# A fourth seven-product pair in each feed-forward layer, alternating PSUM quarters, and transposes one slab behind the square

## The chip, the cores and the metric

The kernel runs on one core of a Trainium2 chip. The metric is the device time of one execution in microseconds (us); for the kernel before, three runs are shown below. One execution was taken with the hardware profiler, and all rows of a trace come from it.

## What is computed

The reference is two residual blocks over 256 tokens of width 2048, in float32. What the change touches is the feed-forward part of the first block's two layers:

```python
D_MODEL = 2048
SEQ = 256
D_FF = 4 * D_MODEL
...
def squared_relu_mlp(h, w1, w2):
    z = jax.nn.relu(h @ w1)
    return (z * z) @ w2
...
        x = x + jnp.concatenate([token_out, mem_out], axis=-1) @ w_out[i]
        x = x + squared_relu_mlp(rms_norm(x, ffn_norm[i]), w_ff1[i], w_ff2[i])
```

The rest is projections, a causal pool, cross attention over a memory, differential attention, and a second block with a gated recurrence and windowed attention.

## The kernel before

**Work.** Every weight matrix is cut into groups of 512 columns, and a group into eight slabs of 256 rows, so that a slab is a 256x512 piece of weights (512 KB). SyncE loads a slab into one of four slots of `raw`. To keep float32 accuracy each slab is split in two parts: ScalarE writes `whi` (a rounded copy, `hi`, L1086) and VectorE writes `wlo` (the rest, `lo`, L1457). The activations lie split in the same way in `set0` and `set1`. TensorE then multiplies high by high, low by high and high by low (L2093 to L2095): for two tiles of rows and two blocks of 128 tokens that is 12 matmuls of 128x512 for a slab. The sums stand in PSUM in `acc0` and `acc1`, in turn by group.

**Order.** `plan()` lists the groups and puts each further step (a sum, a copy, a transpose) behind a numbered slab of an engine. `number_all` makes one stream of tasks of it, and SyncE, ScalarE, VectorE and TensorE all walk through this stream. A task is one load, one split on ScalarE, one split on VectorE, and its matmuls. The load of task n waits until VectorE has split task n-4 (`w_lo`), since there are four slots, and ScalarE's split of task n waits until TensorE has multiplied task n-4.

**The feed-forward part** (`ffn`) has four chunks of 2048 hidden columns a layer. A chunk has four groups of the first product (`w_ff1`), whose outputs are scaled, passed through the relu and squared, transposed, split and stored in `set1`, and four groups of the second (`w_ff2`), which add to `x`.

**Seven-product pairs.** In chunks 1 to 3 the first two groups of the first product are not computed as groups. They are a 2x2 block product (128 tokens by 1024 rows, times 1024 rows by 512 columns), done with seven block products in place of eight. Each block product is a stage (`p1`, `p2`, `p5`, `p3`, `p6`, `p7`, `p4`), each stage four part tasks of six matmuls (L2130 to L2132), and the 28 part tasks of a pair are spread between the ordinary slabs of the chunk before (`pair_of`). The weights of a stage are sums of blocks, which VectorE makes: `chain_sum` (L1472, for `p5`, `p6`, `p4`) adds a loaded block to one of four chain buffers (`qk`, `prob`, two halves of `mkv`), and `u3` (L1464, for `p7`) subtracts. VectorE does this for task n+2 right behind its split of task n, and needs the load of n+2 for it. The four stages `p6`, `p7`, `p4` and `p5` have such a sum for each part; `p1`, `p2`, `p3` have none. The results stand in the four quarters of two PSUM tensors, `tp` and `sd`:

```python
BLOCKS = {"p1": (0, 0), "p2": (1, 0), "p5": (0, 1), "p3": (1, 1), "p6": (1, 1), "p7": (0, 0), "p4": (1, 0)}
...
                ahead = sc.stream[task.n + 2] if task.n + 2 < len(sc.stream) else task
                if ahead.part and ahead.part.stage == "p7":
                    u3(ahead)
                elif ahead.part and ahead.part.stage in ("p5", "p6", "p4"):
                    chain_sum(ahead)
```

**The drain of a pair.** ScalarE copies `p1` to `first_c` and `p5` to `mixed_c`; VectorE adds `p2` and `p6`, then writes two quarters of the output (`part_n2`) and later the two others (`part_n1`). Relu and square on ScalarE, a transpose of 32x32 blocks on VectorE (`turn`, L1648), sixteen small DMAs on GpSimd that finish the transpose (`shuffle`, L1050), and the split into `set1` (`tail`, L1258 on ScalarE and L1630 on VectorE) follow, as for an ordinary group.

## Time and profile before

| | |
|---|---|
| median of 3 runs | 2959.76 us (2959.05 to 2961.48) |
| profiled execution | 2960.76 us, its span 2959.0 us |
| mean granted share of TensorE's clock | 0.998 |
| TensorE busy | 2916.3 us, 99% of the span |
| VectorE busy | 2055.5 us, 69% |
| ScalarE busy | 1616.3 us, 55% |
| GpSimd busy | 634.5 us, 21% |
| HBM read | 598.89 MB |

The busy time of an engine is a sum over its instructions; the time between the start of one matmul and the next is shorter than the duration that a row gives for one, since matmuls overlap. The views that matter beside the page are the chain that ended last, the waits of VectorE, and the windows over single stretches of the feed-forward part.

### The profile page before, as it was taken

Reading aid. Unit: us, or ns where it says so; the run is one execution under the profiler, and the core shown is the slowest. Engines: PE = TensorE matmul, PEld = TensorE weight load, DVE = VectorE, ACT = ScalarE, POOL = GpSimd, SP = SyncE. Lnnn points to the kernel's source line nnn. Section 1 sums busy time; section 2 is a strip of 40 time slices with the busy share of each in tenths; the row PEclk is TensorE's granted clock in tenths of the full one; section 3 lists DMA queues with packets and bytes.
Section 4 is the critical chain, followed back from the end, with each engine's and each line's share of the span. In section 5 each row is a group of like instructions: output and inputs, shape, how many; then the busy total and the mean of one; then the engine's idle time right before and its main releaser. Section 6 shows DMA issues by size and latency. Waiting matters only on the chain.

```text
span 2959.0 us, 35189 instructions
## 1 busy us (share of the span) xinstructions
PE 2916.3 (99%) x12996; PEld 2400.2 (81%) x12996; DVE 2055.5 (69%) x2679; ACT 1616.3 (55%) x2134; POOL 634.5 (21%) x1257
## 2 busy tenths in 40 slices
PE   8999999999999999999999999999999999999998
PEld 7888888888888778788788888888888887878887
DVE  6547777777866777876777777756557777887555
ACT  6435555555554566755555555545444446775433
POOL 0003312213043310013203122133324663100210
PEclk9999999999999999999999999999999999999999
DMA  7546777778777655556777778776876776666774
GB/s 263 165 151 203 237 248 250 246 244 255 243 223 243 205 170 164 164 174 203 228 256 253 251 242 253 246 219 211 239 216 200 219 227 190 207 206 206 249 254 157
DMA packets 358156, 649.53 MB, mean 220 GB/s; under 512 B 38624, under 2 KB 63584, under 8 KB 357216
## 3 DMA queue, kind: packets, MB, share of 16 engines
q1 hardware_dynamic: 312976, 578.89, 61.7%
q0 software_dynamic: 44432, 67.45, 7.2%
q8 instruction: 102, 1.67, 0.3%
q10 hardware_dynamic: 576, 0.94, 0.1%
q14 instruction: 70, 0.57, 0.1%
HBM read 598.89 MB, written 10.49 MB: 206 GB/s over the span
## 4 chain that ended last, share of the span: by engine, by line
PE 73%; DVE 14%; DMA 7%; ACT 4%; issue 2%; DVEq 0%; ACTq 0%
PE acc L2093 21%; PE acc L2095 21%; PE acc L2094 21%; DMA raw<-in_w_ff 6%; DVE wlo L1457 5%; ACT whi L1086 1%; DVE wlo L1450 1%; PE tp L2130 1%; PE tp L2132 1%; PE tp L2131 1%; DVE mkv L1472 1%; DVE ob L1900 1%; PE tp L2299 1%; PE sd L2193 0%; PE sd L2218 0%
## 5 line engine op out<-in xcount | busy, mean ns | idle before, releaser
L1457 DVE TENSOR_TENSOR wlo<-raw,whi 128x1024 fp32r<-128x1024 f32 x920 | 1110.7, 1220 | 548.4 <-ACT whi L1086 544.0
L2093 PE MATMUL acc<-whi,set_hi 128*128 128x512 f32 x3696 | 1459.4, 395 | 20.8 <-DVE wlo L1457 15.4
L2095 PE MATMUL acc<-whi,set_lo 128*128 128x512 f32 x3696 | 1440.3, 390 | 0.0
L2094 PE MATMUL acc<-wlo,set_hi 128*128 128x512 f32 x3696 | 1439.8, 390 | 0.0
L1086 ACT ACTIVATE whi<-raw 128x1024 fp32r<-128x1024 f32 x920 | 959.4, 1057 | 684.1 <-PE acc L2095 378.3
L2093 PEld LDWEIGHTS acc<-whi,set_hi 128*128 128x128 f32 x3696 | 694.8, 188 | 182.8 <-DVE wlo L1457 27.1
L2095 PEld LDWEIGHTS acc<-whi,set_lo 128*128 128x128 f32 x3696 | 694.5, 188 | 146.2
L2094 PEld LDWEIGHTS acc<-wlo,set_hi 128*128 128x128 f32 x3696 | 695.0, 188 | 143.3 <-issue 1.9
L1050 POOL DMA_DIRECT2D u<-u x832 | 406.8, 497 | 1447.5 <-DVE u L1648 1337.9
L1450 DVE SCALAR_TENSOR_TENSOR wlo<-raw,par,whi 128x512 fp32r<-128x512 f32 x160 | 111.7, 747 | 47.1 <-ACT whi L1089 46.3
L1089 ACT ACTIVATE whi<-raw,par 128x512 fp32r<-128x512 f32 x160 | 104.2, 715 | 22.4 <-PE acc L2095 10.9
L1050 POOL DMA_DIRECT2D kv<-kv x112 | 54.9, 499 | 173.2 <-DVE kv L1648 169.1
L1086 ACT ACTIVATE whi<-mkv 128x1024 fp32r<-128x1024 f32 x48 | 50.9, 1061 | 68.0 <-DVE mkv L1472 51.9
L1555 DVE TENSOR_TENSOR x<-acc,x 128x1024 f32<-128x1024 f32 x40 | 48.8, 1220 | 36.3 <-PE acc L2095 36.3
L1457 DVE TENSOR_TENSOR wlo<-mkv,whi 128x1024 fp32r<-128x1024 f32 x48 | 58.4, 1216 | 9.6 <-ACT whi L1086 8.9
L1472 DVE TENSOR_TENSOR mkv<-mkv,raw 128x1024 f32<-128x1024 f32 x36 | 44.0, 1223 | 29.0 <-DMA raw<-in_w_ff 28.9
L1630 DVE TENSOR_TENSOR set_lo<-u,set_hi 128x1024 fp32r<-128x1024 f32 x44 | 53.7, 1220 | 14.4 <-ACT set_hi L1264 12.2
L1648 DVE STREAM_TRANSPOSE u<-stage_b 128x512 f32<-128x512 f32 x80 | 52.0, 688 | 11.2 <-ACT stage_b L1145 11.2
L2130 PE MATMUL tp<-whi,set_hi 128*128 128x512 f32 x144 | 56.0, 389 | 0.0
L2131 PE MATMUL tp<-wlo,set_hi 128*128 128x512 f32 x144 | 56.0, 389 | 0.0
L2132 PE MATMUL tp<-whi,set_lo 128*128 128x512 f32 x144 | 56.0, 389 | 0.0
L1086 ACT ACTIVATE whi<-qk 128x1024 fp32r<-128x1024 f32 x24 | 25.5, 1062 | 48.1 <-DVE qk L1472 33.0
(332 smaller groups left out, 2121.3 us busy)
## 6 DMA issues: line engine op xcount, KB each, us to landing
raw<-in_w_ff SPq DMA_DIRECT2D x560, 512.0 KB, 4.7
raw<-in_w_in SPq DMA_DIRECT2D x248, 512.0 KB, 4.5
raw<-in_w_out SPq DMA_DIRECT2D x96, 512.0 KB, 4.4
u<-u POOLq DMA_DIRECT2D x832, 32.0 KB, 4.2
raw<-in_w_mem_kv SPq DMA_DIRECT2D x32, 512.0 KB, 4.3
raw<-in_w_proj_a SPq DMA_DIRECT2D x32, 512.0 KB, 4.7
raw<-in_w_proj_b SPq DMA_DIRECT2D x32, 512.0 KB, 6.9
raw<-in_w_kv SPq DMA_DIRECT2D x48, 256.0 KB, 3.3
```

The lines of the kernel that those rows point to most:

```text
L1050: dma(to, of).then_inc(sm["shuffled"], 16)
L1086: A_(whi[:, c], src, ACT.Copy).then_inc(w_hi, 1)
L1089: ins = A_(whi[:, c], raw[:, c], ACT.Copy, scale=gain_of(fold, SLAB_K * task.s + t))
L1450: ins = V.scalar_tensor_tensor(out=wlo[:, c], in0=raw[:, c], scalar=gain_of(fold, SLAB_K * task.s + t), in1=whi[:, c].bitcast(f32), op0=AL ...
L1457: V.tensor_tensor(wlo[:, c], src, whi[:, c].bitcast(f32), ALU.subtract).then_inc(w_lo, 1)
L1472: V.tensor_tensor(t, t, raw[:, c], ALU.add).then_inc(sm["chain_add"], 1)
L2093: T.matmul(o, h[:, tok], whi[:, c], start=first, stop=False)
L2094: T.matmul(o, h[:, tok], wlo[:, c], start=False, stop=False)
L2095: ins = T.matmul(o, l[:, tok], whi[:, c], start=False, stop=last)
L2130: T.matmul(bank, h, whi[:, c], start=first, stop=False, skip_group_check=True)
L2131: T.matmul(bank, h, wlo[:, c], start=False, stop=False, skip_group_check=True)
L2132: ins = T.matmul(bank, l, whi[:, c], start=False, stop=last, skip_group_check=True)
```

## The change

In chunks 0 to 3 of a layer the number of pairs is now 0, 1, 1 and 2 (`PAIRS`). The last chunk's first product has no ordinary groups left: two pairs take its four groups, the first over columns 0 to 1023 of the chunk (`col` 0), the second over columns 1024 to 2047. The 56 part tasks of the two lie between the slabs of chunk 2, from 21 slabs before its second product to slab 29 of the 32 of that product (28 part tasks in some 40 slabs for each pair before). Two groups of 8 slabs go and 28 part tasks come, in each of the two layers: the stream grows from 1096 to 1120 tasks, and the matmuls fall by 2 x (192 - 168) = 48. The four groups of the second product in chunk 2 and in chunk 3 are woven in another order, so that the rows of `set1` are free, or needed, in steps.

A pair with an odd number uses the PSUM quarters in another order (`bank`), so that `p1` of a pair only has to wait for `part_n2` of the pair before it, and `p5` for `part_n1`. `part_p1` waits for the relus of the pair before, since it writes `first_c` over.

The transpose of every group and pair (`turn`) now stands a slab behind the square that it reads. Before, the two stood at the same slab in chunk 0, and in the later chunks too for ordinary groups.

```diff
+FF2_LATE = ((0, 1, 2, 3), (4, 5), (6, 7))
+FF2_EVEN = ((0, 1), (2, 3), (4, 5), (6, 7))
+PAIRS = (0, 1, 1, 2)
...
+    def seven(layer, chunk, src, col, first, last):
+
+        p = sc.pair_of(layer, chunk, src, col, first, last)
+        pair = sc.pairs[p]
+        sc.at("act", pair.end("p1") + 5, "part_p1", p)
+        sc.at("dve", pair.end("p2") + 3, "part_c11", p)
+        sc.at("act", pair.end("p5") + 3, "part_p5", p)
+        sc.at("dve", pair.end("p6") + 3, "part_q", p)
+        return p
+
+    def drain(p, of, rst, z, kt, turn, split):
+
+        pair = sc.pairs[p]
+        add = pair.end("p7") + 3
+        if of == "n1":
+            add = max(pair.end("p4") + 3, add + 5)
+        sc.at("dve", add, "part_" + of, p)
+        sc.at("act", add + 2, "relu_" + of, p, rst)
+        sc.at("act", add + 2, "part_square", p, of, sc.staged, sc.tails)
+        sc.turned(max(turn, add + 3), split, ("staged", sc.staged), z, kt)
+        sc.staged += 1
+        if of == "n2":
+            sc.at("act", add + 3, "part_p7", p, sc.staged)
...
-        for c in range(NCHUNK):
-            halved = c > 0
-            gs = [sc.group(f"w_ff1{layer}", 0, D * c + GW * i, a) for i in range(2 if halved else 0, 4)]
+        waiting = []
+        for c, count in enumerate(PAIRS):
+            gs = [sc.group(f"w_ff1{layer}", 0, D * c + GW * i, a) for i in range(2 * count, 4)]
...
             for i, g in enumerate(gs):
-                turn, split = S * (g + 1) + 1, S * (g + 2) + 1
-                if halved:
-                    turn, split = S * (g + 1) + 2, S * (g + 2) + 2
-                sc.at("act", S * (g + 1) + 1, "epi_relu2", g, rst, sc.staged, sc.tails)
-                sc.at("act", turn, "epi_square", g, sc.tails)
-                sc.turned(turn, split, ("staged", sc.staged), z, 4 * i + (8 if halved else 0))
+                e = S * (g + 1)
+                late = 1 if count else 0
+                sc.at("act", e + 1, "epi_relu2", g, rst, sc.staged, sc.tails)
+                sc.at("act", e + 1 + late, "epi_square", g, sc.tails)
+                sc.turned(e + 2 + late, e + 9 + late, ("staged", sc.staged), z, 4 * (2 * count + i))
                 sc.staged += 1
...
+            sc.weave(fs[0], fs[1], FF2_PAIR if count < 2 else FF2_LATE)
+            at_need = ((0, 2), (4, 1), (12, 0)) if count < 2 else ((0, 3), (2, 2), (8, 1), (12, 0))
+            for n, left in at_need:
                 sc.groups[fs[n // S]].need[n % S] = [("tail_lo", sc.tails - left)]
+            more = PAIRS[c + 1] if c < NCHUNK - 1 else 0
+            if more == 1:
+                waiting = [seven(layer, c + 1, a, 0, f - (11, 14, 2)[count if c else 0], f + 26)]
+            elif more == 2:
+                sc.weave(fs[2], fs[3], FF2_EVEN)
+                first, middle = (f - 21, f + 6) if c else (f - 11, f + 9)
+                p = seven(layer, c + 1, a, 0, first, middle - 1)
+                q = seven(layer, c + 1, a, 2 * GW, middle, f + 29)
+                drain(p, "n2", rst, z, 0, f + 11, f + 23)
+                drain(p, "n1", rst, z, 4, f + 24, f + 29)
+                drain(q, "n2", rst, z, 8, f + 31, f + 37)
+                drain(q, "n1", rst, z, 12, f + 38, f + 44)
...
+        quarters = tp[:, 0:GW], tp[:, GW:2 * GW], sd[:, 0:GW], sd[:, GW:2 * GW]
+        def bank(p, stage):
+
+            n = {"p1": 0, "p6": 0, "p4": 0, "p2": 1, "p7": 1, "p5": 2, "p3": 3}[stage]
+            return quarters[(2, 3, 1, 0)[n] if p % 2 else n]
...
                 act.wait_ge(mm, sc.pairs[p].last("p1"))
-                A_(first_c[:], bank_a, ACT.Copy).then_inc(sm["part_p1"], 1)
+                if p:
+                    act.wait_ge(sm["part_relu"], 2 * p)
+                A_(first_c[:], bank(p, "p1"), ACT.Copy).then_inc(sm["part_p1"], 1)
...
                     if stage == "p1" and p:
+                        pe.wait_ge(sm["part_n2"], p)
+                    elif stage == "p5" and p:
                         pe.wait_ge(sm["part_n1"], p)
```

Two places of VectorE's order show how the instructions move. The first is the stage `p4` of a pair in layer 0, in which `qk`, `prob` and `mkv` are the chain buffers, the rows `qk<-qk,raw` and the like are the sums, and each `wlo` is the split of one task. Before (the pair of chunk 2):

```order
L1472 TENSOR_TENSOR qk<-qk,raw 128x1024
L1457 TENSOR_TENSOR wlo<-raw,whi 128x1024
L1457 TENSOR_TENSOR wlo<-qk,whi 128x1024
L1457 TENSOR_TENSOR wlo<-raw,whi 128x1024
L1472 TENSOR_TENSOR prob<-prob,raw 128x1024
L1457 TENSOR_TENSOR wlo<-raw,whi 128x1024
L1525 TENSOR_TENSOR stage_a<-sd,scan 128x512
L1526 TENSOR_TENSOR stage_a<-tp,scan 128x512
L1457 TENSOR_TENSOR wlo<-prob,whi 128x1024
L1472 TENSOR_TENSOR mkv<-mkv,raw 128x1024
```

With the change (the second pair of chunk 3):

```order
L1505 TENSOR_TENSOR qk<-qk,raw 128x1024
L1490 TENSOR_TENSOR wlo<-raw,whi 128x1024
L1490 TENSOR_TENSOR wlo<-qk,whi 128x1024
L1505 TENSOR_TENSOR prob<-prob,raw 128x1024
L1490 TENSOR_TENSOR wlo<-raw,whi 128x1024
L1490 TENSOR_TENSOR wlo<-prob,whi 128x1024
L1505 TENSOR_TENSOR mkv<-mkv,raw 128x1024
L1490 TENSOR_TENSOR wlo<-raw,whi 128x1024
L1558 TENSOR_TENSOR stage_a<-tp,scan 128x512
L1559 TENSOR_TENSOR stage_a<-sd,scan 128x512
```

Between one sum and the next there were two splits or three; now there are always two, since every ordinary task has a part task behind it, and at some places two part tasks stand together.

The second place is the transpose of the second group in chunk 0 of layer 0, where `sum_lo` is the split of a sum of activations, `set_lo<-u` the tail of the group before, and `u<-stage_b` the transpose. Before, and then with the change:

```order
L1457 TENSOR_TENSOR wlo<-raw,whi 128x1024
L1507 TENSOR_TENSOR sum_lo<-prob,sum_hi 128x1024
L1630 TENSOR_TENSOR set_lo<-u,set_hi 128x1024
L1648 STREAM_TRANSPOSE u<-stage_b 128x4x4x32 x2
L1457 TENSOR_TENSOR wlo<-raw,whi 128x1024
L1507 TENSOR_TENSOR sum_lo<-qk,sum_hi 128x1024
```

```order
L1490 TENSOR_TENSOR wlo<-raw,whi 128x1024
L1540 TENSOR_TENSOR sum_lo<-prob,sum_hi 128x1024
L1663 TENSOR_TENSOR set_lo<-u,set_hi 128x1024
L1490 TENSOR_TENSOR wlo<-raw,whi 128x1024
L1540 TENSOR_TENSOR sum_lo<-qk,sum_hi 128x1024
L1681 STREAM_TRANSPOSE u<-stage_b 128x4x4x32 x2
```

The transpose went behind the next split and the last `sum_lo`.

## Rows read from the trace of the kernel before

**Rows 1.** The page: span, and busy time of each engine.
```profile
span 2959.0 us, 35189 instructions
PE 2916.3 (99%) x12996; PEld 2400.2 (81%) x12996; DVE 2055.5 (69%) x2679; ACT 1616.3 (55%) x2134; POOL 634.5 (21%) x1257
```

**Rows 2.** The page: the chain that ended last, by engine and by line.
```profile
PE 73%; DVE 14%; DMA 7%; ACT 4%; issue 2%; DVEq 0%; ACTq 0%
PE acc L2093 21%; PE acc L2095 21%; PE acc L2094 21%; DMA raw<-in_w_ff 6%; DVE wlo L1457 5%; ACT whi L1086 1%; DVE wlo L1450 1%; PE tp L2130 1%; PE tp L2132 1%; PE tp L2131 1%; DVE mkv L1472 1%; DVE ob L1900 1%; PE tp L2299 1%; PE sd L2193 0%; PE sd L2218 0%
```

**Rows 3.** Windows: stretch, its length, busy time of each engine, clock, DMA share.
```profile
core 0: us, PE busy (x) PEld busy (x) DVE busy (x) ACT busy (x) POOL busy (x), PEclk, DMA share, GB/s
577.90:644.80 66.90, 66.30 (x293) 54.57 (x291) 54.26 (x49) 34.50 (x35) 0.00 (x0) 1.00 0.71 239
747.10:813.50 66.40, 66.40 (x295) 54.92 (x293) 54.39 (x50) 35.54 (x36) 0.00 (x0) 1.00 0.71 241
343.00:412.00 69.00, 69.00 (x306) 57.11 (x306) 50.48 (x46) 42.38 (x44) 15.63 (x32) 1.00 0.82 263
```

**Rows 4.** Timeline of TensorE: start, length, line and tiles of each matmul.
```profile
577.62 0.39 PE L2094 MATMUL acc<-wlo,set_hi 128*128 128x512 f32 x1
...
581.48 0.39 PE L2130 MATMUL sd<-whi,sum_hi 128*128 128x512 f32 x1
```

**Rows 5.** Timeline of VectorE in a stage with sums; idle time in brackets.
```profile
576.65 1.22 DVE L1457 TENSOR_TENSOR wlo<-raw,whi 128x1024 fp32r<-128x1024 f32 x1
585.60 1.23 DVE L1472 TENSOR_TENSOR prob<-prob,raw 128x1024 f32<-128x1024 f32 x1 [1.33 <-DMA raw<-in_w_ff]
...
591.28 1.22 DVE L1457 TENSOR_TENSOR wlo<-raw,whi 128x1024 fp32r<-128x1024 f32 x1
...
609.65 0.69 DVE L1519 TENSOR_TENSOR scan<-tp,scan 128x512 f32<-128x512 f32 x1
610.25 1.22 DVE L1555 TENSOR_TENSOR x<-acc,x 128x1024 f32<-128x1024 f32 x1
```

**Rows 6.** Waits of VectorE from 577.9 to 644.8: us, times, longest.
```profile
DVE mkv L1472 <- DMA raw<-in_w_ff: 3.8, 2, 2.1
DVE prob L1472 <- DMA raw<-in_w_ff: 3.6, 2, 2.3
DVE raw L1464 <- DMA raw<-in_w_ff: 2.5, 2, 1.5
DVE qk L1472 <- DMA raw<-in_w_ff: 2.3, 2, 1.7
DVE wlo L1457 <- ACT whi L1086: 0.5, 1, 0.5
```

**Rows 7.** Loads at L915 from 577.9 to 644.8, then at L900 from 343 to 412.
```profile
DMA to landing us min/median/max: 3.6/4.6/5.8
DMA to landing us min/median/max: 3.6/5.1/6.9
```

**Rows 8.** Timelines where that stretch ends: VectorE's late split, and TensorE behind it.
```profile
643.60 1.22 DVE L1457 TENSOR_TENSOR wlo<-raw,whi 128x1024 fp32r<-128x1024 f32 x1
644.87 0.50 PE L2093 MATMUL acc<-whi,set_hi 128*128 128x512 f32 x1 [0.67 <-DVE wlo L1457]
```

**Rows 9.** Timelines around two transposes: chunk 0 of layer 0, chunk 0 of layer 1.
```profile
326.39 1.31 DVE L1648 STREAM_TRANSPOSE u<-stage_b 128x512 f32<-128x512 f32 x2 [0.91 <-ACT stage_b L1145]
327.62 1.18 DVE L1457 TENSOR_TENSOR wlo<-raw,whi 128x1024 fp32r<-128x1024 f32 x1
328.86 0.50 PE L2093 MATMUL acc<-whi,set_hi 128*128 128x512 f32 x1 [1.97 <-DVE wlo L1457]
1473.91 1.30 DVE L1648 STREAM_TRANSPOSE u<-stage_b 128x512 f32<-128x512 f32 x2
1476.38 0.50 PE L2093 MATMUL acc<-whi,set_hi 128*128 128x512 f32 x1 [0.93 <-DVE wlo L1457]
```

**Rows 10.** TensorE at 1416 us, timeline, and the window behind it.
```profile
1416.42 0.50 PE L2093 MATMUL acc<-whi,set_hi 128*128 128x512 f32 x1 [1.98 <-DVE wlo L1457]
1416.90:1420.30 3.40, 3.40 (x10) 2.65 (x9) 2.87 (x3) 0.00 (x0) 3.40 (x8) 0.50 0.60 133
```

**Rows 11.** The page: GpSimd's issues of a shuffle, and their landing.
```profile
L1050 POOL DMA_DIRECT2D u<-u x832 | 406.8, 497 | 1447.5 <-DVE u L1648 1337.9
u<-u POOLq DMA_DIRECT2D x832, 32.0 KB, 4.2
```

More of the change, by code:

```diff
@@ L101, with __init__ @@
 class Pair:
-    def __init__(self, layer, chunk, src, first):
-        self.layer, self.chunk, self.src, self.first = layer, chunk, src, first
+    def __init__(self, layer, chunk, src, col, first):
+        self.layer, self.chunk, self.src, self.col, self.first = layer, chunk, src, col, first
         self.parts = {}
@@ L132, in __init__, with pair_of @@
         self.stream = []
-    def pair_of(self, layer, chunk, src, first, last):
+    def pair_of(self, layer, chunk, src, col, first, last):
         p = len(self.pairs)
-        pair = Pair(layer, chunk, src, not any(q.layer == layer for q in self.pairs))
+        pair = Pair(layer, chunk, src, col, not any(q.layer == layer for q in self.pairs))
         self.pairs.append(pair)
@@ L388, in ffn @@
                     sc.at("dve", v + (14, 15, 17, 18)[n], "sum_lo", layer, n)
[L389 removed]
+            elif count == 1:
                 v = S * gs[0]
[L391 to L401 removed]
@@ L412, in ffn @@
-            if c < NCHUNK - 1:
-                v = S * fs[0]
-                p = sc.pair_of(layer, c + 1, a, v - (14 if halved else 12), v + 26)
-                pair = sc.pairs[p]
-                sc.at("act", pair.end("p1") + 3, "part_p1", p)
-                sc.at("dve", pair.end("p2") + 3, "part_c11", p)
-                sc.at("act", pair.end("p5") + 3, "part_p5", p)
-                sc.at("dve", pair.end("p6") + 3, "part_q", p)
-            for n, left in ((0, 2), (4, 1), (12, 0)):
-                sc.groups[fs[n // S]].need[n % S] = [("tail_lo", sc.tails - left)]
+            f = S * fs[0]
@@ L830, in block_of @@
             pair = sc.pairs[part.pair]
-            row, col = P * (k * NK // 2 + SLAB_K * part.j), D * pair.chunk + GW * (1 - n)
+            row, col = P * (k * NK // 2 + SLAB_K * part.j), D * pair.chunk + pair.col + GW * (1 - n)
             return W[f"w_ff1{pair.layer}"][row:row + SLAB_K * P, col:col + GW].rearrange("(t p) n -> p t n", p=P)
@@ L1532, in part_n1 @@
                 t = stage_a[:, GW:2 * GW]
-                V.tensor_tensor(t, bank_a, t, ALU.add).then_inc(sm["part_n1"], 1)
+                V.tensor_tensor(t, bank(p, "p4"), t, ALU.add).then_inc(sm["part_n1"], 1)
             def rms(dst, ssq, n, count):
@@ L2112, in part_slab @@
                 p, stage = part.pair, part.stage
-                bank = {"p1": bank_a, "p6": bank_a, "p4": bank_a, "p2": bank_b, "p7": bank_b, "p5": bank_c,
-                        "p3": bank_d}[stage]
+                o = bank(p, stage)
                 fresh = stage not in ("p6", "p4")
@@ L2129, in part_slab @@
                     last = part.j == QUARTERS - 1 and t == SLAB_K - 1
-                    T.matmul(bank, h, whi[:, c], start=first, stop=False, skip_group_check=True)
-                    T.matmul(bank, h, wlo[:, c], start=False, stop=False, skip_group_check=True)
-                    ins = T.matmul(bank, l, whi[:, c], start=False, stop=last, skip_group_check=True)
+                    T.matmul(o, h, whi[:, c], start=first, stop=False, skip_group_check=True)
+                    T.matmul(o, h, wlo[:, c], start=False, stop=False, skip_group_check=True)
+                    ins = T.matmul(o, l, whi[:, c], start=False, stop=last, skip_group_check=True)
                 ins.then_inc(mm, 1)
```

29 lines of the change are left out of this document (9 added, 20 removed).

## The prediction

> **What bounds the kernel now.** I read the page first. The span is 2959.0 us, and TensorE is busy in 99% of it [rows 1]. In the chain that ended last, TensorE has 73%; the next entries are the loads `raw<-in_w_ff` with 6% and VectorE's split `wlo` with 5%, both from the feed-forward part [rows 2]. So TensorE sets the pace, and it is at some places handed its weights just in time by a loop of load, sum, split. Then I read the windows over the two stretches of layer 0 in which the stages p6, p7 and p4 of chunk 2's and chunk 3's pair run: TensorE is busy in 66.30 of 66.90 us and in all of 66.40 [rows 3]. The timeline gives its pace: from 577.62 to 581.48 us 17 matmuls start, 0.227 us apiece [rows 4]. An ordinary task of 12 is thus 2.72 us, a part task of 6 is 1.36 us, in pair stages as elsewhere.
>
> The same stretch shows what is nearly as slow. VectorE is busy 54.26 of 66.90 us, and most of the rest, 12.2 us, are eight waits for a load in front of one of its 12 sums, 1.0 us a sum on average; only 0.5 us is waiting for ScalarE [rows 3, 6]. TensorE has 29 tasks there, 17 x 2.72 + 12 x 1.36 = 62.6 us of matmuls, so VectorE's walk through them was 4.3 us slower than TensorE's. It was paid from a lead: the split of the first part task ended at 576.65 + 1.22 = 577.87, and TensorE came to it at 581.48, 3.6 us later [rows 4, 5]. At the end the lead is gone and TensorE stands still for 0.67 us [rows 8]. The lead is bounded by the four slots and grows again in stages without sums. A pair thus costs nothing now only because each stage with sums ends when the lead does.
>
> **The change, part by part.**
>
> *Matmuls.* 48 fewer at 0.227 us is **-10.9 us**. They lie on TensorE, which is full [rows 3], so all of it counts unless TensorE then waits.
>
> *VectorE with alternating tasks.* Back to back, VectorE starts an instruction every (591.28 - 585.60) / 5 = 1.136 us, and a 512-wide PSUM addition takes 0.60 us [rows 5]; a transpose takes 1.23 us from its start to the split behind it [rows 9]. First pair of the last chunk, p6 to p4: 23 splits and 12 sums are 39.8 us, with two transposes, one tail and three PSUM additions 45.2 us. TensorE needs 11 x 2.72 + 12 x 1.36 = 46.2 us. Second pair: 22 splits and 12 sums are 38.6 us, with one transpose, one tail and three additions 42.8 us, against 43.5 us of matmuls. By its work alone VectorE keeps up, barely; before, it had 54.3 against 62.6.
>
> The waits decide. A sum needs a load that starts when the split four tasks earlier is done. Now two splits (2.27 us) often stand between them and a load takes 4.6 us [rows 7], hence waits of up to 2.3 [rows 6]. With strict alternation a sum and two splits stand between, 3.41 us. What is short of the landing is then shared by two successive sums, since a wait at one also gives the next load more time. In the stretches before, GpSimd moved nothing; in the new ones it runs two shuffles, and where shuffles run now the median landing is 5.1 us, not 4.6 [rows 3, 7]. I take 5.0: (5.0 - 3.41) / 2 = 0.8 us a sum. Where another instruction stands between, the wait is covered: five of twelve sums in the first pair, four in the second. That leaves 5.6 and 6.4 us, and 0.5 us each for ScalarE as now. First pair: 45.2 + 5.6 + 0.5 - 46.2 = 5.1 us behind; second: 42.8 + 6.4 + 0.5 - 43.5 = 6.2. A lead of 3.6 us was there before; I take 3.0 for both, as p5 with its sums comes shortly before and p3 has less ordinary work to recover in. TensorE waits 2.1 + 3.2, and 0.4 in the two stages p5: 5.7 us a layer, **+11.4 us** in all. The bounds: with no wait at all both stages end with lead left, 0. With 1.0 us for each of the 12 sums, none covered, the pairs are 11.5 and 11.8 us behind, 17.3 us after the leads, with 2 more in p5 19.3 a layer or +38.6. I stay nearer the first, since the wait now comes from the places with two splits only.
>
> A page of the Trainium skill, "DMA: Bandwidth & Descriptors", section "Anatomy of one DMA", gives a fixed 2.0 us and the bytes at 436 GB/s, for a load issued by GpSimd; for 512 KB that is an estimate of 3.2 us. By it no sum would wait, and the kernel would gain the full 10.9 us. These loads are issued by SyncE, and none in the stretch landed in under 3.6 us [rows 7].
>
> *Transposes one slab later.* In chunk 0 of each layer VectorE waited for ScalarE's square (0.91 us at 326.39) and TensorE then stood 1.97 us; at 1473.91 a transpose in front of the split helped to make TensorE wait 0.93 us [rows 9]. Behind the split, the second wait should go and the first lose little, as `sum_lo` and the transpose now stand before the next split. Between -3.9 and +1 I take **-1.0 us**. The shuffle starts a slab later: sixteen issues of 0.50 and a landing of 4.2 us are 12.2 us [rows 11], against seven slabs (19 us) or, for the last pair, six (16.3 us). That is covered, with 4 us to spare; past that the last tail would hold TensorE.
>
> *At nothing.* ScalarE's 24 more splits and as many more loads: ScalarE is busy 34.50 of 66.90 us, the DMAs 0.71, and 0.82 is seen without loss [rows 3]. The quarters cost no instruction; `p1` and `p5` of the next pair are multiplied after the additions they wait for stand in VectorE's order, and without the alternation `p1` would wait for `part_n1`. The new wait of `part_p1` is for relus that ScalarE has behind it.
>
> **Sum.** 2960.76 (profiled execution) - 10.9 + 11.4 - 1.0 = 2960.3. The median of the runs is 1.0 below the profiled one: **2959.3 us, no change**. A measurement of this kernel can tell 0.2%, 5.9 us, from no change.
>
> **Rivals.**
>
> *The loads land in time: faster.* If landings stay near the minimum of 3.6 to 4.2 us [rows 7], the wait is 0.1 to 0.4 us a sum, and with 3 us of lead hardly 1 us a layer reaches TensorE: 2959.8 - 10.9 - 1.0 + 2 = 2950. For it: less than half the loads would be issued directly behind another. Against it: both medians.
>
> *The loop of load, sum and split takes over: slower.* If the landing is 5.6 us, as the larger ones now are, a sum waits 1.1 us, and 7 and 8 uncovered sums put the pairs 7.2 and 8.9 us behind; less 3.0 each, plus 1 in p5, 11.1 a layer, +22.2: 2959.8 - 11.9 + 22.2 = 2970. It decides from 8.9 us a layer on. For it: loads come closer together, two part tasks stand together at some places, ScalarE has relus and squares in the first pair's stages. Against it: waits at neighbouring sums overlap.
>
> *The clock falls.* At 1416 us TensorE, after 1.98 us without a matmul, ran at 0.50 of its clock, the level of 1.2 GHz, for 3.4 us: eight to ten matmuls at 0.43 us cost 1.6 us; the equal wait of 1.97 us in layer 0 did not do it [rows 9, 10]. If half of some twelve new waits are that long and each brings it, it adds 10 us: 2969. The waits I expect are under 1.5 us each. The Trainium skill, "TensorE: Matmul & The Clock Gate", Part 1, says that an idle array is gated to half its clock and that activity releases it; the trace agrees at 1416 us.
>
> *The order does not do what it says:* TensorE waits for a pair's additions or the last tail, so that the 10.9 us are replaced by one wait a layer; 2955 to 2965.
>
> **Chances.** Forecast (waits of 3 to 8.9 us a layer) 0.34, time 2954 to 2966; loads in time 0.31; loop takes over 0.27; clock 0.05; last rival 0.03. Together: faster 0.31, same 0.36, slower 0.33. The forecast's own range is 2954 to 2966; the whole range, leaving a tenth out on either side, is 2949 to 2976.
>
> **What would show it.** In the profile after: 48 matmuls fewer, and in each layer's last two pairs VectorE without idle time but in front of L1505 and L1497, behind `raw<-in_w_ff`, some 0.5 us a sum over all. TensorE's idle time behind `wlo` should stand at the ends of p4 in both pairs, more in the second, 5 to 6 us a layer. The wait at the third transpose of layer 1's chunk 0 should be gone. I am wrong if TensorE stays full in these stages, if a wait stands elsewhere (a tail, a transpose, the relu of a pair), or if the granted clock falls there.

## The result, and the profile after

| | before | after |
|---|---|---|
| median of 5 runs, us | 2959.50 | 2977.11 |
| lowest and highest, us | 2958.54, 2961.48 | 2975.57, 2979.74 |
| span of the profiled execution, us | 2959.0 | 2974.6 |

The changed kernel takes 1.0059 of the time of the kernel before, 95% interval 1.0044 to 1.0074. It is slower by 17.6 us, where no change was forecast. The page of the kernel after, its span, busy times and chain:

```profile
span 2974.6 us, 35299 instructions
PE 2917.7 (98%) x12948; PEld 2387.5 (80%) x12948; DVE 2126.0 (71%) x2745; ACT 1645.6 (55%) x2164; POOL 636.3 (21%) x1257
PE 67%; DVE 17%; DMA 9%; ACT 4%; issue 3%; DVEq 0%; ACTq 0%; SPq 0%
PE acc L2126 19%; PE acc L2128 19%; PE acc L2127 19%; DMA raw<-in_w_ff 8%; DVE wlo L1490 7%; ACT whi L1117 2%; DVE wlo L1483 1%; DVE mkv L1505 1%; PE sd L2166 1%; PE sd L2165 1%; PE sd L2164 1%; PE tp L2166 1%; PE tp L2165 1%; PE tp L2164 1%; DVE raw L1497 1%
raw<-in_w_ff SPq DMA_DIRECT2D x576, 512.0 KB, 4.6
```

The 48 matmuls are gone (12996 became 12948 [rows 1]). In the chain TensorE gave up 6 points, from 73% to 67%, and VectorE and the loads took them [rows 2]. What was L1457, L1472, L1464 and L1086 before is L1490 (split `wlo`), L1505 (sum), L1497 (difference for `p7`) and L1117 (`whi`) now.

The windows show where the time went. The first and last are the stretches of a layer's last two pairs, from the first `p1` task to three slabs behind the last `p4` task; between them stand, of layer 0, `p5` of the first pair, its p6 to p4 with one slab behind, `p1` and `p2` of the second pair, and its p6 to p4 with two slabs behind:

```profile
core 0: us, PE busy (x) PEld busy (x) DVE busy (x) ACT busy (x) POOL busy (x), PEclk, DMA share, GB/s
653.40:888.70 235.30, 226.77 (x973) 180.70 (x973) 191.49 (x175) 136.31 (x142) 45.73 (x94) 1.00 0.81 257
683.80:701.20 17.40, 16.89 (x74) 13.40 (x73) 12.90 (x12) 8.46 (x9) 5.52 (x12) 1.00 0.88 274
717.50:769.60 52.10, 50.41 (x217) 40.13 (x216) 44.51 (x42) 28.99 (x30) 15.67 (x32) 1.00 0.81 257
769.60:798.80 29.20, 28.04 (x121) 22.30 (x121) 20.36 (x19) 18.63 (x20) 7.83 (x16) 1.00 0.81 265
831.10:885.70 54.60, 51.37 (x216) 39.51 (x216) 46.50 (x45) 29.88 (x31) 9.62 (x20) 1.00 0.74 241
1750.40:1982.80 232.40, 226.11 (x974) 180.92 (x973) 192.14 (x175) 136.50 (x142) 46.35 (x95) 1.00 0.82 260
```

Do not read the stall off the busy column. It leaves 8.5 us idle in the first stretch, but rows overlap: a matmul lasts 0.39 us by its row and the next one starts after 0.227, so the first 0.16 us of every wait is covered, and the matmul behind a wait is drawn longer (0.50 us [rows 8, 9]). Count instead: at the pace of 0.2267 us a matmul (0.227 in [rows 4]; 220.30 us for 972 where nothing stalls, in a_fifth below) its 972 matmuls are 220.4 us, and it took 235.3. TensorE lost **14.9 us** there, and 12.0 in layer 1: **26.9 us** where the forecast has 11.4. By the same count, with the ends of tasks from the trace (layer 0 and 1): p6 to p4 of the first pair 3.2 and 3.9, of the second 5.7 and 4.4; the two stages `p5` 2.7 and 2.1; the stages `p1` to `p3` 3.1 and 1.7. By this count the whole feed-forward part of both layers had 12.2 us of stalls before, 2.0 of them in the stretches of chunk 2's and chunk 3's pairs; now there are 11.2 us outside the last two pairs. So -10.9 + 26.9 + 11.2 - 12.2 = +15.0 us, against 15.6 in the spans.

What VectorE waited for between 650 and 900 us:

```profile
DVE wlo L1490 <- ACT whi L1117: 28.2, 28, 2.3
DVE mkv L1505 <- DMA raw<-in_w_ff: 5.9, 6, 1.8
DVE prob L1505 <- DMA raw<-in_w_ff: 4.4, 4, 2.3
DVE qk L1505 <- DMA raw<-in_w_ff: 4.2, 3, 2.3
DVE raw L1497 <- DMA raw<-in_w_ff: 3.6, 3, 1.6
```

That is 18.1 us for loads, in 16 waits in front of 32 sums and differences; they are no longer than those of [rows 6]. The kernel before had 16.5 us of such waits between 650 and 880 us, in front of the 16 sums and differences of a single pair, and TensorE lost nothing there. In the stretches of chunk 2's and chunk 3's pairs of both layers it lost 2.0 us before; in those of the last two pairs it now loses 26.9. One round of a raw buffer in the second pair shows why. Its rows in the timelines of SyncE's queue, VectorE, ScalarE and TensorE (start, length, idle time in brackets):

```profile
829.25 0.37 SPq L946 DMA_DIRECT2D raw<-in_w_ff  x1
...
828.00 1.23 DVE L1490 TENSOR_TENSOR wlo<-qk,whi 128x1024 fp32r<-128x1024 f32 x1
829.14 1.22 DVE L1505 TENSOR_TENSOR prob<-prob,raw 128x1024 f32<-128x1024 f32 x1
830.28 1.22 DVE L1490 TENSOR_TENSOR wlo<-raw,whi 128x1024 fp32r<-128x1024 f32 x1
831.49 1.23 DVE L1490 TENSOR_TENSOR wlo<-prob,whi 128x1024 fp32r<-128x1024 f32 x1
833.83 1.23 DVE L1505 TENSOR_TENSOR mkv<-mkv,raw 128x1024 f32<-128x1024 f32 x1 [1.11 <-DMA raw<-in_w_ff]
834.97 1.22 DVE L1490 TENSOR_TENSOR wlo<-raw,whi 128x1024 fp32r<-128x1024 f32 x1
836.18 1.22 DVE L1490 TENSOR_TENSOR wlo<-mkv,whi 128x1024 fp32r<-128x1024 f32 x1
...
835.09 1.06 ACT L1117 ACTIVATE whi<-mkv 128x1024 fp32r<-128x1024 f32 x1 [2.17 <-DVE mkv L1505]
...
830.91 0.39 PE L2164 MATMUL sd<-whi,sum_hi 128*128 128x512 f32 x1
```

The split at 828.00 ends at 829.23 and gives the buffer back; the load is issued at 829.25 and has landed at 833.8; the sum ends at 835.06, ScalarE's `whi` at 836.15, the split at 837.40: 8.15 us, and the next load into that buffer starts. 4.6 of them are the load (the median), 3.6 the sum and the two splits, with nothing in between. TensorE works in the same time through the four tasks that the four buffers hold: two ordinary and two of a part, 8.16 us. The round is as long as the work it feeds. Before, with fewer part tasks per slab, the four tasks ahead of each part task in p6 to p4 of chunk 2's and chunk 3's pairs were three ordinary and one of a part: 9.52 us. The lead is short as well: TensorE begins at 830.91 what was split at 829.23, 1.7 us after.

### The profile page after: what moved, and what is told of

The parts are those of the page before. It is cut to its first block, busy times and chain, and to the rows that moved or that the text cites. A ratio compares the mean times of both kernels' runs of the same rounds, so it can differ in the third digit from the quotient of the medians.

```text
span 2974.6 us, 35299 instructions
## 1 busy us (share of the span) xinstructions
PE 2917.7 (98%) x12948; PEld 2387.5 (80%) x12948; DVE 2126.0 (71%) x2745; ACT 1645.6 (55%) x2164; POOL 636.3 (21%) x1257
## 4 chain that ended last, share of the span: by engine, by line
PE 67%; DVE 17%; DMA 9%; ACT 4%; issue 3%; DVEq 0%; ACTq 0%; SPq 0%
PE acc L2126 19%; PE acc L2128 19%; PE acc L2127 19%; DMA raw<-in_w_ff 8%; DVE wlo L1490 7%; ACT whi L1117 2%; DVE wlo L1483 1%; DVE mkv L1505 1%; PE sd L2166 1%; PE sd L2165 1%; PE sd L2164 1%; PE tp L2166 1%; PE tp L2165 1%; PE tp L2164 1%; DVE raw L1497 1%
## 5 line engine op out<-in xcount | busy, mean ns | idle before, releaser
L1490 DVE TENSOR_TENSOR wlo<-raw,whi 128x1024 fp32r<-128x1024 f32 x912 | 1102.2, 1220 | 512.9 <-ACT whi L1117 509.2
L2126 PE MATMUL acc<-whi,set_hi 128*128 128x512 f32 x3568 | 1414.1, 396 | 33.4 <-DVE wlo L1490 26.9
L2128 PE MATMUL acc<-whi,set_lo 128*128 128x512 f32 x3568 | 1391.0, 390 | 0.0
L2127 PE MATMUL acc<-wlo,set_hi 128*128 128x512 f32 x3568 | 1390.2, 390 | 0.0
L1117 ACT ACTIVATE whi<-raw 128x1024 fp32r<-128x1024 f32 x912 | 950.9, 1058 | 643.5 <-PE acc L2128 343.5
L2126 PEld LDWEIGHTS acc<-whi,set_hi 128*128 128x128 f32 x3568 | 670.6, 188 | 205.9 <-DVE wlo L1490 51.0
L2128 PEld LDWEIGHTS acc<-whi,set_lo 128*128 128x128 f32 x3568 | 670.3, 188 | 141.8
L2127 PEld LDWEIGHTS acc<-wlo,set_hi 128*128 128x128 f32 x3568 | 671.0, 188 | 136.8 <-issue 1.9
L1117 ACT ACTIVATE whi<-mkv 128x1024 fp32r<-128x1024 f32 x64 | 68.0, 1062 | 98.1 <-DVE mkv L1505 82.4
L1490 DVE TENSOR_TENSOR wlo<-mkv,whi 128x1024 fp32r<-128x1024 f32 x64 | 78.0, 1219 | 13.4 <-ACT whi L1117 13.1
L1505 DVE TENSOR_TENSOR mkv<-mkv,raw 128x1024 f32<-128x1024 f32 x48 | 58.7, 1223 | 23.9 <-DMA raw<-in_w_ff 23.6
L1588 DVE TENSOR_TENSOR x<-acc,x 128x1024 f32<-128x1024 f32 x40 | 48.7, 1219 | 28.2 <-PE acc L2128 28.2
L1117 ACT ACTIVATE whi<-prob 128x1024 fp32r<-128x1024 f32 x32 | 33.9, 1060 | 49.6 <-DVE prob L1505 38.8
L1117 ACT ACTIVATE whi<-qk 128x1024 fp32r<-128x1024 f32 x32 | 34.0, 1061 | 41.5 <-DVE qk L1505 24.9
L2164 PE MATMUL sd<-whi,sum_hi 128*128 128x512 f32 x128 | 50.0, 391 | 0.8 <-DVE wlo L1490 0.8
L2165 PE MATMUL sd<-wlo,sum_hi 128*128 128x512 f32 x128 | 49.8, 389 | 0.0
```

The source lines that it names most:

```text
L1117: A_(whi[:, c], src, ACT.Copy).then_inc(w_hi, 1)
L1490: V.tensor_tensor(wlo[:, c], src, whi[:, c].bitcast(f32), ALU.subtract).then_inc(w_lo, 1)
L1505: V.tensor_tensor(t, t, raw[:, c], ALU.add).then_inc(sm["chain_add"], 1)
L2126: T.matmul(o, h[:, tok], whi[:, c], start=first, stop=False)
L2127: T.matmul(o, h[:, tok], wlo[:, c], start=False, stop=False)
L2128: ins = T.matmul(o, l[:, tok], whi[:, c], start=False, stop=last)
```

## Experiments

Every ratio is against the kernel before, measured beside the run, with its 95% interval. "Stalls" are TensorE's in the two stretches of the last two pairs, counted as above: 26.9 us in the changed kernel.

### Is it the fourth pair?

```diff
 # a_three: the change with three pairs, as before
-PAIRS = (0, 1, 1, 2)
+PAIRS = (0, 1, 1, 1)
```

> The changed kernel with three pairs a layer, PAIRS = (0, 1, 1, 1): alternating quarters, later transposes and the new drain stay, the fourth pair goes. If the fourth pair's stretch is the cause of all, 2958 to 2961. If the alternation or the new places of the drain cost something too, above 2963.

Measured: 2961.11 us, 0.9998 (0.9989 to 1.0007). The alternating quarters, the new drain and the later transposes cost nothing that can be measured. The whole loss comes with the fourth pair.

### Give the buffer back earlier

```diff
 # a_early: SyncE's wait before a load into the slot of task n - 4
-sp.wait_ge(w_lo, task.n + 1 - RAW)
+slot_free(sp, task.n - RAW)   # behind the sum if that was p5, p6 or p4
```

> The changed kernel, but the load of task n no longer waits for the split of task n-4 where that task is a part of p5, p6 or p4 (its slot is free once VectorE's sum has read it) or of p1 (which uses no slot): SyncE waits for the sum instead. Work of every engine is unchanged. Theory 1 (sums wait for loads that start too late, because a slot is given back only by the split): the idle time of VectorE in front of its sums in the last two pairs falls to under a third, TensorE's idle time in these stretches falls from about 27 us to under 9, time 2977 - 18 = 2959 or less. Theory 2 (VectorE's work alone is too much where part tasks alternate with slabs): the stalls stay, time 2973 to 2978.

Measured: 2966.01 us, 1.0016 (1.0008 to 1.0025), stalls 17.2: between the two theories, and neither had it. The 11 us gained show that the time at which loads start matters. VectorE's waits for loads fell only from 18.1 to 15.9 us: the ordinary slabs' buffers still come back as late as before.

> The same edit of SyncE's wait in the kernel before. Theory 1: before had a lead that paid for the waits, so that only its 3 us of small stalls at the ends of p4 can go: 2957, at most 4 us less than before. Theory 2: no difference, 2959 to 2960.

The same edit on the kernel before: 2958.71 us, 0.9994 (0.9985 to 1.0003). Without the fourth pair it gained nothing that can be measured.

### The transposes

```diff
 # b_turn: the kernel before, its ordinary transposes a slab later
-sc.turned(turn, split, ("staged", sc.staged), z, ...)
+sc.turned(turn + 1, split, ("staged", sc.staged), z, ...)
```

> The kernel before with every transpose of an ordinary feed-forward group one slab later, and nothing else. My prediction's term: 1 us less (2958.5). Rival, from the stalls in chunk 0 of layer 0, which grew from 3.2 to 5.5 us: the transpose now stands behind the last split of a sum and costs there, 1 to 3 us more in layer 0, and gives 1 to 2 back in layer 1.

```diff
 # a_turnback: the change, its transposes a slab earlier
-sc.turned(e + 2 + late, e + 9 + late, ...)
+sc.turned(e + 1 + late, e + 9 + late, ...)
```

> The change, but the ordinary groups' transposes back at one slab behind their group's end, beside the square, as in the kernel before. By the measurement on the kernel before (chunk 0 lost 1 to 3 us by the later place): chunk 0's stalls fall from 10.4 to near 8 us in the two layers, time 2973 to 2976. If the later place is what the two pairs' stretches need (the order of VectorE's and ScalarE's work there), their stalls rise over 26.9 and the time over 2980.

Measured: b_turn 2962.51 us, 1.0004 (0.9995 to 1.0013); a_turnback 2976.03 us, 1.0053 (1.0037 to 1.0069). Both are too near their neighbours to tell. In b_turn the stalls in chunk 0's first product rose from 3.2 and 4.8 us to 5.5 and 5.5, and the later one of layer 1 fell from 1.9 to 0.5. The timeline of VectorE in b_turn at the place of [rows 9]:

```profile
325.10 1.22 DVE L1630 TENSOR_TENSOR set_lo<-u,set_hi 128x1024 fp32r<-128x1024 f32 x1
328.18 1.23 DVE L1457 TENSOR_TENSOR wlo<-raw,whi 128x1024 fp32r<-128x1024 f32 x1 [1.86 <-ACT whi L1086]
329.32 1.22 DVE L1507 TENSOR_TENSOR sum_lo<-qk,sum_hi 128x1024 fp32r<-128x1024 f32 x1
330.45 1.30 DVE L1648 STREAM_TRANSPOSE u<-stage_b 128x512 f32<-128x512 f32 x2
331.68 2.32 DVE L1457 TENSOR_TENSOR wlo<-raw,whi 128x1024 fp32r<-128x1024 f32 x2
```

ScalarE has relu and square in front of its split. Before, VectorE did the transpose while ScalarE made `whi`; now it waits 1.86 us for `whi` (0.91 for the square before) and still has the transpose ahead of the next split. TensorE's wait at this place did not grow by it: the next matmul starts 2.05 us late at 329.46, 2.13 us late at 328.86 before. The 2.3 us more in layer 0 are two new small waits (0.37 us at 307.96 and 0.14 at 321.83, with 0.11 behind each) and, most of it, the clock. The windows from 330.80 to 334.30 in b_turn, then in the kernel before:

```profile
330.80:334.30 3.50, 3.50 (x10) 2.72 (x9) 3.19 (x4) 0.00 (x0) 2.00 (x5) 0.51 0.71 205
330.80:334.30 3.50, 3.50 (x17) 2.89 (x16) 1.41 (x2) 0.39 (x1) 3.50 (x8) 1.00 0.93 287
```

The granted clock fell to 0.50, the level of 1.2 GHz, for 3.4 us there, which cost 1.6 us (eight matmuls that each took 0.20 us more). In layer 1 it fell in both, as in [rows 10]. So b_turn says little of the place of the transpose: over both layers its stalls rose by 1.8 us, and 1.6 of them are this fall.

### Shorten the round in three ways

```diff
 # a_blind: the sums read and wait for no load; ScalarE's split waits for it (the difference for p7 stays)
-dve.wait_ge(ld[task.slot], 16 * task.loads)
-V.tensor_tensor(t, t, raw[:, c], ALU.add)
+V.tensor_tensor(t, t, t, ALU.max)
 # a_half_sum: 512 of the 1024 columns of each sum and difference
-V.tensor_tensor(t, t, raw[:, c], ALU.add)
+c = slice(c.start, c.start + GW)
+V.tensor_tensor(t[:, 0:GW], t[:, 0:GW], raw[:, c], ALU.add)
 # a_half_load: one of the two row tiles of the blocks of p5, p6, p7, p4
+to, of = to[:, 0:1], of[:, 0:1]
```

> The change, but VectorE's 7 sums of a part with a loaded block take the chain's own buffer twice and no longer wait for the load; ScalarE's split of the part waits for it instead. VectorE does the same number of elements, and the sums' values are left out of the computation. Theory 1 (VectorE's waits for loads that start only when a slot is given back are the loss): VectorE's waits for transfers between 650 and 900 us fall from 18.1 to under 5 us, TensorE's stalls in the two stretches of the last two pairs from 26.9 to under 10 us, time near 2960. Theory 2 (VectorE's own work in the part stages is more than TensorE's): the waits vanish, but the stalls stay over 20 us and the time over 2970. Theory 3 (VectorE and ScalarE wait for each other in turn, and the load only starts it): stalls between, 12 to 18 us, time near 2966.

> The change, but every sum of a part with a loaded block and the difference for the second operand cover 512 of 1024 columns: VectorE has about 0.6 us less to do per part task, the waits are those of the change, the left columns' sums are left out of the computation. Theory 2 (VectorE's own work): stalls of TensorE in the stretches of the last two pairs fall from 26.9 us to under 12, time near 2960 or below. Theory 1 (the loads): VectorE only waits longer for the same loads; stalls stay over 18 us, time 2968 to 2975, VectorE's waits for transfers rise over 18.1 us between 650 and 900 us.

> The change, but the loads of the parts of p5, p6, p7 and p4 bring one of the two row tiles (256 KB where it was 512), so half of these blocks' values are left out of the computation. All waits and all work on the engines stay. Theory 1 (the time from slot given back to landed, 4.6 to 5.1 us median, is the loss): landings come about 0.6 to 1 us sooner, stalls in the last two pairs' stretches fall from 26.9 to 14 to 20 us, time 2964 to 2969. Theory 2: under 3 us of change, 2974 to 2977.

| | us | ratio | stalls | VectorE's waits for loads, 650 to 900 |
|---|---|---|---|---|
| a_blind | 2960.76 | 0.9998 (0.9989 to 1.0008) | 11.4 | 5.7 |
| a_half_sum | 2962.50 | 1.0011 (1.0001 to 1.0020) | 13.9 | 28.9 |
| a_half_load | 2951.25 | 0.9969 (0.9956 to 0.9982) | 3.7 | 5.5 |

a_blind came out near what the first theory said (11.4 us for under 10); the two others fit none of the theories. a_half_sum gained 15 us while VectorE waited longer for loads, so the length of those waits is no measure of the loss. a_half_load gained 26 us, not 8 to 13, and was faster than the kernel before. The page of a_half_load gives the landings:

```profile
raw<-in_w_ff SPq DMA_DIRECT2D x448, 512.0 KB, 4.5
raw<-in_w_ff SPq DMA_DIRECT2D x128, 256.0 KB, 3.1
```

What the three have in common is the round: shorter by a sum's half (0.6 us), by a sum that runs beside the load, or by 1.4 us of landing. Each takes about half of the 26.9 us of stalls or more. That is the second rival of the text on record: the loop of load, sum and split is the bound, and every piece of it counts. But VectorE's work in a_half_sum and the bytes in a_half_load went down too, so two other causes were left: VectorE's own work, and the throughput of the DMA engines.

### Loosen the order instead

```diff
 # a_free: p1 parts take no raw buffer; buffers go to the least recently used
+if not (part and part.stage == "p1"):
+    t.raws = min(range(RAW), key=lambda i: (used[i], i))
 # a_spread2: parts further apart
-waiting = [seven(layer, c + 1, a, 0, f - (11, 14, 2)[count if c else 0], f + 26)]
+waiting = [seven(layer, c + 1, a, 0, f - (11, 21)[min(c, 1)], f + (26, 16)[min(c, 1)])]
-first, middle = (f - 21, f + 6) if c else (f - 11, f + 9)
+first, middle = (f - 31, f + 5)
 # a_spread_early2: with a_early's slot_free; a_spread_free: with both
```

> The change, but a part of p1, whose block goes straight into the chain's buffer, no longer takes a place in the ring of four raw buffers: loads around p1 find a buffer one task sooner. Nothing else differs. If the loop raw buffer given back, load, sum, split is what stalls the last two pairs (the loop theory; the half loads took 26 us off, the half sums 15, the sums that don't wait 16), the stretches of p1 and p2 and the p5 behind them gain: stalls there fall from 26.9 to 20 to 24 us and the time is 2969 to 2974. If only VectorE's own amount of work counts, nothing changes: 2975 to 2978.

> The change, with the parts of chunk 2's pair and of the last two pairs set further apart: chunk 2's pair from 21 slabs before to 16 behind the start of chunk 1's second product (was 14 and 26), the last two pairs from 31 before to 29 behind chunk 2's (was 21), the border between them one slab sooner, and the first one's n2 added at the earliest 4 slabs behind. The same work, waits and buffers. If the density of parts is the cause (more than one part per ordinary slab makes VectorE's work longer than TensorE's), the stalls in the last pairs' stretches fall from 26.9 to about 15 us, with 2 to 3 new ones in chunk 2's pair, time 2963 to 2968. If it is the latency of each load alone, whatever the density, the stalls stay over 22 and the time over 2971.

> a_spread2 with the raw buffer given back when the sum has read it, as in a_early, where that took 11 us off. If the two act on the same loop and each still helps, the stalls in the last pairs' stretches are 6 to 10 us and the time 2954 to 2959, at or below the kernel before. If the rest of a_early's stalls (17 us) is VectorE's own work in dense stretches, spreading takes most of it; if it is the loads of the ordinary slabs, it stays: 2962 to 2966.

> All three together: parts further apart, raw buffer given back behind the sum, p1 without a raw buffer. Candidate for a version that beats both kernels. The floor of TensorE's work allows 10.9 us below the kernel before, less what the later transposes cost in chunk 0 (1 to 3): 2950 to 2957 if the loop was the whole cause, as with the half loads (2951).

Measured: a_free 2978.78 us, 1.0061 (1.0048 to 1.0074), stalls 27.5: no gain, a miss. Of these 27.5 us, 1.6 are a fall of the clock at 695.67 us; why the rest stayed no run shows. a_spread2 2973.42 us, 1.0051 (1.0039 to 1.0063), a miss too: the last two pairs lost 18.3 us from their first to their last part task, but the pairs of chunk 2, now denser, 5.4 where they had lost nothing. The second pair of chunk 3 is as dense as it was, and from p6 to p4 it still lost 4.3 and 5.6 us. a_spread_early2 2967.39 us, 1.0021 (1.0012 to 1.0030), and a_spread_free 2965.06 us, 1.0018 (1.0009 to 1.0027): both above what was expected, and no better than a_early alone within the intervals. a_spread_early2 ran from 2959.9 to 2972.1 us, and its profiled execution was its fastest, so its trace is not used here. That such a kernel moves with the scatter of the landings is likely and not shown. Setting parts apart did not settle anything: the density could be lowered in one stretch only at the cost of another.

### A fifth buffer

A fifth raw buffer leaves the bytes, VectorE's work and the order as they are, and gives the round five tasks in place of four. Parts of `p1` take no raw buffer in it, as in a_free, where that alone gained nothing. It fits over the parameter row (read at the start) and the rope scratch, which nothing uses in the feed-forward part; it is in use from the first pair's first part to the end of chunk 2's second product.

```diff
 # a_fifth (b_fifth: the same on the kernel before)
+fifth = nc.alloc_sbuf_tensor_at("fifth", [P, SLAB], f32, offset=...)   # over row, rtmp, rqs
+lent = any(a <= v < b for a, b in self.wide)
+t.raws = min(range(RAWS if lent else RAW), key=lambda i: (used[i], i))
+self.free[t.n], used[t.raws] = used[t.raws], t.n
-sp.wait_ge(w_lo, task.n + 1 - RAW)
+sp.wait_ge(w_lo, sc.free[task.n] + 1)
```

> The change with a fifth raw buffer from the first pair's first part to the end of chunk 2's second product in each layer; parts of p1 take none. It lies over the parameter row and the rope scratch, which nothing reads there; all loads, sums, splits and products are the change's. The loop from a raw buffer given back to the split of what is loaded into it then spans five tasks (about 10 us of TensorE's work in the last pairs' stretch) where it spanned four (8). If the loop of four buffers is the cause of the new stalls: VectorE's waits for transfers between 650 and 900 us fall from 18.1 to under 5 us, the last pairs' stalls from 26.9 to under 8, time 2950 to 2956, below the kernel before. If the DMA engines' throughput is the cause (they were 75% busy there), a fifth buffer only lets the loads queue longer: median landing rises from 4.7 to over 6 us, the waits stay over 12, the time over 2970. If VectorE's own work is: the waits vanish but stalls of 15 or more stay, time over 2963.

> The kernel before with the same fifth raw buffer over the same stretches. Its stalls in the feed-forward stretches are 12.2 us in all, of which only 2.5 in those of the pairs (the rest in the first chunk, before the buffer is there), so the loop theory gives at most 1 to 3 us: 2957 to 2960. If a fifth buffer helped the kernel before by 5 or more, the gain in a_fifth would be no evidence on the change.

> a_fifth with the raw buffer also given back behind the sum, as in a_early. If the loop is off the bound with five buffers, this adds under 2 us either way (2949 to 2956). If a_fifth keeps stalls over 8 us that come from loads, this takes some of them.

| | us | ratio |
|---|---|---|
| a_fifth | 2947.71 | 0.9958 (0.9945 to 0.9970) |
| b_fifth | 2955.07 | 0.9986 (0.9977 to 0.9994) |
| a_fifth_early | 2949.13 | 0.9960 (0.9947 to 0.9974) |

The windows of a_fifth: the first and last row are the two stretches, as 653.40:888.70 and 1750.40:1982.80 in the kernel after; between them p6 to p4 of each pair in layer 0, as 717.50:769.60 and 831.10:885.70.

```profile
651.50:871.80 220.30, 220.30 (x973) 182.49 (x972) 190.82 (x175) 137.21 (x142) 45.77 (x94) 1.00 0.83 267
714.00:763.00 49.00, 49.00 (x218) 40.59 (x217) 44.50 (x42) 31.01 (x32) 15.67 (x32) 1.00 0.88 282
820.10:869.10 49.00, 49.00 (x217) 40.57 (x217) 46.46 (x45) 29.85 (x30) 11.32 (x24) 1.00 0.79 253
1733.50:1953.90 220.40, 220.40 (x973) 182.43 (x973) 190.41 (x175) 136.69 (x142) 45.73 (x94) 1.00 0.82 268
```

The stalls are gone, all 26.9 us. VectorE is as busy as before in the stretch (190.8 us, 191.5 in the kernel after), so its own work is not the cause. The DMA engines move more (267 GB/s, 257 after) at a share of 0.83, so their throughput was not the limit. VectorE's waits for loads, in a_fifth, between 650 and 900 us:

```profile
DVE raw L1522 <- DMA raw<-in_w_ff: 1.0, 2, 0.6
DVE mkv L1529 <- DMA raw<-in_w_ff: 0.9, 2, 0.5
```

Nor did the loads become quicker: from 651.5 to 871.8 us the part loads took

```profile
DMA to landing us min/median/max: 3.6/4.7/10.8
```

with the same median as in the kernel after (3.6/4.7/7.3) and a longer tail. b_fifth gained 4.5 us, more than the 1 to 3 expected. In its profiled execution the stalls of all six pairs are gone, 4.4 us, those of chunk 1's pairs included; another 1.6 us are missing because the clock did not fall in layer 1's chunk 0 (1.00 from 1410 to 1430 us), where the fifth buffer isn't in use. So of a_fifth's 11.9 us below the kernel before, the buffer and that chance give 4.5, and the fourth pair 7.4 on top, where its matmuls are 10.9. The difference is mostly the later transposes: a_fifth has 3.2 us more of stalls in chunk 0's first products than b_fifth, and the clock fell in neither before 2900 us. Giving the buffer back early adds nothing any more.

The last run puts the transposes back in a_fifth, where no stall of the pairs hides what they do.

> a_fifth with the ordinary groups' transposes back at one slab behind their group's end, beside the square, as before the change. With four buffers the place was worth 1 to 3 us of stalls in chunk 0 (b_turn: TensorE's stalls there rose by 3.0 us over both layers, w_ff21's fell by 1.4; a_turnback: no more than 1 us in all). If the later place costs what b_turn showed, this is 1 to 2 us faster than a_fifth: 2945.5 to 2947. If it pays, as the prediction had it (1.0 us), 2948.5 to 2950.

Measured: 2945.87 us, 0.9950 (0.9936 to 0.9964), **1.8 us less than a_fifth** and 15 below the kernel before. The intervals of the two overlap, so the times alone do not decide. The traces do: the clock fell in neither before 2900 us, and the stalls in chunk 0's first product are 3.1 and 3.5 us, a_fifth's 4.6 and 4.9; 1.1 us of new stalls in the last two pairs' stretches take a part of it back. TensorE's waits between 277 and 480 us, in a_fifth_back:

```profile
PE acc L2150 <- DVE wlo L1515: 2.0, 1, 2.0
```

and in a_fifth:

```profile
PE acc L2150 <- DVE wlo L1515: 2.5, 3, 1.9
```

a_fifth_back has the lowest median of this study, and is ahead of both kernels.

## Why the prediction was wrong

*The matmuls, -10.9 us: right.* 48 fewer, at the pace given; with the waits away (a_fifth against b_fifth) 7.4 us of it are seen in the time.

*VectorE with alternating tasks, +11.4 us: mis-sized, the step that failed.* The mechanism, loads that start when a buffer is given back and a lead that pays for the waits, was the right one, and the part tasks of two pairs cost 26.9 us by it. The walk of VectorE from p6 to p4 came out close to the working. Counted as the text counted it, VectorE fell behind TensorE by 4.9 and 6.2 us in the first pairs of the two layers (5.1 forecast), and by 9.0 and 6.0 in the second (6.2). Its waits for loads there were 13.6 and 11.8 us a layer, against 5.6 + 6.4. What failed is the lead:

- "I take 3.0 for both." At the task at which the text read 3.6 us, the last of p3, the lead was 1.9 and 2.9 us in layer 0 and 2.5 and 1.9 in layer 1: 9.2 us where 12.0 were counted on. With that and the second pair of layer 0, TensorE waited 3.2 to 3.9 us in the first pairs' p6 to p4 and 4.4 to 5.7 in the second, for 2.1 and 3.2: 6.6 us more than forecast.
- "0.4 in the two stages p5." Measured 2.7 and 2.1: 4.0 us more over both layers. The lead at the first p5 task was 1.4 to 1.8 us, where chunk 2's and chunk 3's pair had 2.6 and 2.9 in layer 0 before.
- `p1` to `p3`, at nothing: 3.1 and 1.7 us. There is no sum there, but in p1 and p2 of the second pairs the lead was down to 0.05 us several times, so a transpose, tail or relu reached TensorE. In layer 0 ScalarE's square waits for VectorE's transpose until 789.00, and VectorE's split then 2.14 us for ScalarE.

So more than half of the missing 15.5 us fell outside the stages for which the sum was made. The sum for the round shows beforehand that the lead would not come back: 4.6 + 1.2 + 1.1 + 1.2 = 8.1 us and the hand-overs (load, sum, ScalarE's split with its mean of 1.06 us by the page of before, VectorE's split), against 2 x 2.72 + 2 x 1.36 = 8.16. A lead grows only where the round is shorter than TensorE's four tasks; in the kernel before it rose to 4.2 us in p1 or p2 of each of chunk 2's and chunk 3's pairs, now to 3.4 at most. VectorE's waits for loads do not tell the loss either: a_half_sum had 28.9 us of them and half the stalls.

*Transposes one slab later, -1.0 us: wrong in sign where it can be seen.* Chunk 0's first products have 2.9 us more of stalls with it, and the time is 1.8 us longer (a_fifth against a_fifth_back); with four buffers the effect stayed below what can be measured. The wait for the square went, and a longer one for ScalarE's split came (1.86 for 0.91 us), with the transpose still to do. The wait in layer 1's chunk 0, 0.93 us, did go as forecast.

*At nothing:* the quarters and the drain: right (a_three). ScalarE's and the queues' work: right, by a_fifth, which has all of it and no stall in these stretches.

*The rivals.* The loop of load, sum and split took over, given 0.27 and 2970 us. Its mark, 8.9 us a layer, was passed with 12 to 15. It was priced with a landing of 5.6 us; the median stayed at 4.7, and the time came out 7 us above that rival and 1 above the range. (With its eight waits of 1.1 us the second pair is 8.6 us behind and not 8.9, which changes its price by 0.6 us.) The loads in time (2950) are what a_half_load and a_fifth made of it. The clock did not fall in these stretches (granted clock 1.00 in every window of the kernel after above). Elsewhere in the feed-forward part it fell once: at 330.93 us in layer 0's chunk 0, for 3.4 us, where the kernel before kept it, and not in layer 1's, where the kernel before lost it; the two cancel. The order did what it said.

*What would show it:* idle time at the ends of p4 was seen, and more in the second pair in layer 0 (2.8 us for 2.0), not in layer 1 (0.8 for 1.7, with 2.4 in p7). That VectorE would stand idle only before L1505 and L1497 held from p6 to p4 and not outside, where it waited for ScalarE's split, 28.2 us between 650 and 900 (47.7 before, between 650 and 880).

## What to carry to other kernels

For work that is fed through a ring of buffers, compare the round of one buffer (given back, loaded, worked on, given back) with the time the consumer needs for as many tasks as there are buffers. Here late loads cost next to nothing as long as the first was well below the second; when the change brought them together, each term of the round that was shortened took half of the loss or more away, and the producer's waits for loads did not tell how much. A forecast that pays such waits from a lead has to show where the lead is won back. Then look for one more buffer before touching the order: a scratch area idle in that stretch was worth 29 us here, where the changes to the order and to the release of a buffer were worth 12 at most.

## What the runs showed of the hardware

- A stalled TensorE is in part invisible in its busy time: 8.5 us idle in a stretch where counting matmuls at 0.2267 us shows 14.9. Where nothing stalls the two agree (220.30 us busy in 220.30).
- A wait of TensorE of 2.0 to 2.2 us in chunk 0 was followed by a fall of the granted clock to 0.50 for 3.4 us in some profiled executions and not in others: in the kernel before in layer 1 alone, in the kernel after in layer 0 alone, in b_turn in both, in a_fifth and b_fifth in neither. A fall costs 1.6 us, as much as the effects that were looked for there, so the clock has to be read before two such stretches are compared.
- With more on the DMA engines the landings took longer. With a share of 0.88 and 282 GB/s (a_fifth, 714 to 763 us) part loads landed in a median of 4.9 us and slabs in 5.9, the longest in 11.6; in the kernel after, with 0.81 and 257 GB/s (717.5 to 769.6 us), in 4.4 and 4.3, the longest in 6.4. TensorE lost nothing by it there (49.00 us busy in 49.00).
- Halving a load to 256 KB took 1.4 us off its landing, from 4.5 to 3.1 us, less than half. A straight line through the two medians leaves 1.7 us that do not depend on the size, an estimate. The Trainium skill, "DMA: Bandwidth & Descriptors", section "Anatomy of one DMA", has for a load issued by GpSimd a fixed 2.0 us and the bytes at 436 GB/s: by it an estimate of 3.2 and 2.6 us. For these loads of SyncE the runs have both longer, the large one most.
